# Twelve RMS norms: the inverse root moves from ScalarE and VectorE to one power operation on GpSimd

## What is computed

```python
def rmsnorm(t, g, eps=RMS_EPS):
    tf = t.astype(jnp.float32)
    tf = tf * lax.rsqrt(jnp.mean(tf * tf, axis=-1, keepdims=True) + eps)
    return (tf * g.astype(jnp.float32)).astype(t.dtype)

h = h + rmsnorm(m, g[1])                               # mixer's output
f = sq_relu_mlp(rmsnorm(h, g[2]), mlp_w1[i], mlp_w2[i])
h = h + rmsnorm(f, g[3])
```

## Time and profile before

| what | value |
|---|---|
| runs (median, lowest, highest) | 1945.8 us, 1937.51, 1949.15 |
| profiled execution, its own time | 1939.3 us |
| its span, first to last instruction | 1937.5 us |
| TensorE busy | 1656.3 us, 85% |
| VectorE busy | 1117.8 us, 58% |
| ScalarE busy | 746.8 us, 39% |
| GpSimd busy | 107.3 us, 6% |
| granted TensorE clock, mean | 0.90 |

### The profile page before, as it was taken

The page is one execution under the profiler, slowest core; times in us unless marked ns, Lnnn a source line. Parts: engine busy times, 40 slices in busy tenths (PEclk is TensorE's granted clock), DMA queues, the critical chain, the costliest instruction groups (busy, mean ns, idle before and its releaser), DMA issues. The chain is left out here.

```text
span 1937.5 us, 36240 instructions
## 1 busy us (share of the span) xinstructions
PE 1656.3 (85%) x15007; PEld 1565.6 (81%) x15007; DVE 1117.8 (58%) x1813; ACT 746.8 (39%) x1000; POOL 107.3 (6%) x139
## 2 busy tenths in 40 slices
PE   3899989947888988999887788579998889779997
PEld 2899989927878987999886786579998875579997
DVE  6995457968795556444465652654434446655444
ACT  1554345731002634554345000346533434346532
POOL 0011000002120000110000210000000020000000
PEclk7899999959999998999988696789999995589998
DMA  9897545402233454665442000225453430125551
GB/s 303 242 315 223 174 141 174 152 0 85 93 90 112 139 174 120 179 189 174 153 140 67 2 2 2 85 90 173 158 170 113 152 116 1 44 95 188 169 179 44
DMA packets 297019, 252.87 MB, mean 131 GB/s; under 512 B 9032, under 2 KB 295597, under 8 KB 296893
## 3 DMA queue, kind: packets, MB, share of 16 engines
q1 hardware_dynamic: 296589, 249.96, 42.0%
q10 hardware_dynamic: 304, 1.11, 0.1%
HBM read 249.99 MB, written 1.05 MB: 130 GB/s over the span
## 5 line engine op out<-in xcount | busy, mean ns | idle before, releaser
L399 DVE TENSOR_TENSOR w_lo<-raw,w_hi 128x2048 fp32r<-128x2048 f32 (+2 forms) x203 | 456.4, 2250 | 538.6 <-ACT w_hi L391 538.3
L466 PE MATMUL bank<-x_hi,w_hi 128*128 128x256 f32 (+1 forms) x2224 | 647.7, 291 | 72.6 <-DVE x_lo L660 41.4
L468 PE MATMUL bank<-x_hi,w_lo 128*128 128x256 f32 (+1 forms) x2224 | 639.0, 287 | 0.0
L467 PE MATMUL bank<-x_lo,w_hi 128*128 128x256 f32 (+1 forms) x2224 | 638.9, 287 | 0.0
L391 ACT ACTIVATE w_hi<-raw 128x2048 fp32r<-128x2048 f32 (+2 forms) x203 | 381.6, 1880 | 457.8 <-PE bank L468 419.3
L466 PEld LDWEIGHTS bank<-x_hi,w_hi 128*128 128x128 f32 x2224 | 428.1, 192 | 82.3 <-issue 69.7
L468 PEld LDWEIGHTS bank<-x_hi,w_lo 128*128 128x128 f32 x2224 | 429.8, 193 | 0.0
L467 PEld LDWEIGHTS bank<-x_lo,w_hi 128*128 128x128 f32 x2224 | 428.1, 193 | 0.9 <-issue 0.7
L466 PE MATMUL bank<-mh_hi,w_hi 128*128 128x272 f32 (+1 forms) x512 | 148.3, 290 | 6.5 <-PEq L2016 6.5
L467 PE MATMUL bank<-mh_lo,w_hi 128*128 128x272 f32 (+1 forms) x512 | 147.5, 288 | 0.0
L468 PE MATMUL bank<-mh_hi,w_lo 128*128 128x272 f32 (+1 forms) x512 | 147.3, 288 | 0.0
(11 more groups left out here) (432 smaller groups left out, 2160.4 us busy)
## 6 DMA issues: line engine op xcount, KB each, us to landing
raw<-in_mlp_w SPq DMA_DIRECT2D x128, 512.0 KB, 4.4
raw<-in_w_ffn_up SPq DMA_DIRECT2D x88, 512.0 KB, 5.2
raw<-in_w_ada SPq DMA_DIRECT2D x72, 512.0 KB, 4.8
raw<-in_w_in SPq DMA_DIRECT2D x60, 512.0 KB, 4.7
raw<-in_w_ffn_down SPq DMA_DIRECT2D x32, 512.0 KB, 4.5
raw<-in_od_w_in SPq DMA_DIRECT2D x24, 512.0 KB, 4.5
raw<-in_ev_w_in SPq DMA_DIRECT2D x18, 512.0 KB, 4.7
raw<-in_w_ffn_down SPq DMA_DIRECT2D x16, 384.0 KB, 3.8
```

Of the source, the lines that this page charges most:

```text
L399: nc.vector.tensor_tensor(w_lo[:, s_at % 2, 0:kt], raw[:, r_at % RING, 0:kt], w_hi[:, s_at % 2, 0:kt].bitcast(F32), ALU.subtract).then_inc ...
L466: nc.tensor.matmul(out, hi, xh[:, k0 + k, 0:L], start=start, stop=False)
L467: nc.tensor.matmul(out, hi, xl[:, k0 + k, 0:L], start=False, stop=False)
L468: mm = nc.tensor.matmul(out, lo, xh[:, k0 + k, 0:L], start=False, stop=stop)
```

## The change

`Norm` gets a method for GpSimd. After VectorE has written mean square plus epsilon, GpSimd raises it to the power minus one half in one TENSOR_TENSOR operation, whose second operand is a column filled once with -0.5 and broadcast along the row. It writes straight to where the refined root stood and raises `n_y`. The ACTIVATE of line 631 and, for these norms, the call of `inverse_root` go. VectorE waits for `n_y` as before. Each of the blocks that hold a norm gets a GpSimd part (the diff shows two of them).

```diff
+        half_neg = sb("half_neg", [P, 1])
...
+            @block.gpsimd
+            def _(pool):
+                nc.gpsimd.memset(half_neg[:], -0.5)
...
+            def on_pool(self, pool):
+
+                pool.wait_ge(n_ms, self.q + 1)
+                nc.gpsimd.tensor_tensor(stat[:, 3, 0:self.L], stat[:, 0, 0:self.L], half_neg.broadcast_to([P, self.L]), ALU.pow).then_inc(n_y, 1)
+
             def on_act(self, act, mid=None, between=None):
 
                 L = self.L
-                act.wait_ge(n_ms, self.q + 1)
-                nc.scalar.activation(stat[:, 1, 0:L], stat[:, 0, 0:L], ACT.Abs_reciprocal_sqrt).then_inc(n_y, 1)
                 if between:
                     between()
...
                 nc.vector.tensor_scalar(stat[:, 0, 0:L], banks[6][:, 0:L], 1.0 / D, EPS, ALU.mult, ALU.add).then_inc(n_ms, 1)
-                inverse_root(dve, n_y, self.q + 1, stat[:, 0, 0:L], stat[:, 1, 0:L], stat[:, 2, 0:L], stat[:, 3, 0:L])
+                dve.wait_ge(n_y, self.q + 1)
                 for n in range(DT + 2):
...
                                                     hid_hi[:, bass.ds(n, 1)].bitcast(F32), ALU.subtract).then_inc(hid_l, 1)
+                        norm.on_pool(pool)
                         each_pair(pool, FF1T, 2, body)
...
+                @block.gpsimd
+                def _(pool):
+                    if before:
+                        before.on_pool(pool)
+                    if norm:
+                        norm.on_pool(pool)
```

More of the change, by code:

```diff
@@ L905, in _ @@
                 nc.scalar.activation(sp_t[:, 2], sp_t[:, 1], ACT.Exp, scale=-1.0).then_inc(ba_act, 1)
+            @block.gpsimd
+            def _(pool):
+                norm_mix.on_pool(pool)
             @block.vector
@@ L1498, in _ @@
                         norm_in.square(act, u, sq)
+                @block.gpsimd
+                def _(pool):
+                    norm_final.on_pool(pool)
                 @block.vector
@@ L1650, in _ @@
             def _(pool):
+                norm_in.on_pool(pool)
                 pool.wait_ge(q["bon"], 1)
```

## The result

The changed kernel takes 2413.6 us (median of four runs, 2409.5 to 2416.3), the kernel before 1945.6 us beside it. The ratio is 1.242 (1.2383 to 1.2457): 468.0 us slower, where 35 us were forecast and 161 us was the upper bound. The sign was right; the change in time was wrong by a factor of thirteen.

What follows compares the result with a forecast made beforehand. TensorE's stream of products and the stretches where it stands still were taken to bound the kernel. Terms 57.9 + 8.6 - 29.6 - 1.3 - 0.5 = +35.1 us on 1939.3 gave 1974 us; range 1927 to 2100 us.

Steps and rivals of the forecast that it cites:

- The sign: Whole kernel: slower than before, by +35.1 us; slower by over 1% had chance 0.64.
- What bounds it: All twelve norms: TensorE waits, so mean square to first scaled tile is on the path one for one.
- Break-even: Twelve norms: the change breaks even where the powers cost 22.8 us in all, 1.9 us each.
- The interval before: Twelve norms of the old kernel, mean square to first scaled tile: 2.29 to 3.08 us each, sum 29.6 us.
- The interval without the power: Twelve changed norms: mean square and hand-overs to and from GpSimd, 0.71 us each, 8.6 in all (7.9 to 9.7).
- The power: GpSimd at twelve norms: 4.7 us over 256 positions, 5.0 over 272, 57.9 us in all (10.7 to 183.8).
- Rival 3: GpSimd's power: steps wait for one another, 10 us or more each; with 14.9 us, +161, 2100 us; chance 0.27.
- The other terms: Outside the norms: -1.3 us in the RWKV mixer, -0.5 in the first up loop, nothing in the second.
- the mixer's table load: RWKV mixer: load ahead of the rows TensorE awaits goes, everything behind comes 1.28 us sooner, -1.3 us.
- the up loops: Two up projections: 22 table loads go, 28 us of ScalarE's time; -0.5 us in the first, nothing in the second.
- rival 4: Up projections: table loads count for more, loops gain 28 us; with a power as cheap as a product, 1899 us; chance 0.03.
- TensorE's clock: Behind norms: a longer wait can move the return to full clock; nothing counted, 6 us either way allowed.

Runs made afterwards that it cites:

- the quarter power: Changed kernel with GpSimd raising only the first 64 positions, ScalarE and VectorE doing the others the old way: 2042.8 us against 1941.3, ratio 1.0535.

## Why the prediction was wrong, point by point

**What bounds it: right.** The interval from mean square to first scaled tile was said to be on the path one for one at all twelve norms. Three kernels with intervals of 14.0, 133.9 and 512.8 us bear that out. Only the gains of the kernels without refining steps (16.8 us of intervals for 6 and for 10 us of time) fall short of one for one. Break-even was put at 1.9 us a power: a product of 0.61 us won, the quarter power of 10.53 lost, and nothing in between was run. (The prediction says that even a free power can't win over 1%; its own -22.8 us are 1.2%, and the product in the power's place did win 1.2%.)

**The interval before: right.** 29.6 us.

**The interval without the power: a little high.** 0.71 us was counted for mean square and hand-overs, 0.54 to 0.55 was measured: 0.08 us to GpSimd rather than the 0.19 of the earlier trace rows, 0.04 back rather than 0.1. Twelve times, 2.1 us.

**The power: this step failed, and with it the whole number.** The text took 24 arithmetic steps at the price of one stream each, 0.77 ns per element, and got 4.7 and 5.0 us; and it took 24 steps at a whole product's price, 14.9 and 15.9 us, as the upper bound. Measured are 41.12 and 43.70. The term of 57.9 us is 506.3. Per element of a row that is 161 ns, 209 streams of 0.77 ns; in products of this run (0.614 us) a power is 67 of them. So neither the price of a step nor its bound held. Two things were wrong in it. The count of 24 steps came from no row, and both the forecast and the upper end of the range hung on it, so that they weren't independent; and the reasoning took the rate of products, which the earlier trace rows show as a rate of streams, for the rate at which a function of many steps is worked off. What the earlier trace rows could bound was the price from below. From above they bound nothing.

**Rival 3** (steps that wait for one another, 10 us or more) had the right direction and 0.27 of the chance, but its price was 14.9 us, not 41. Whether the steps inside the power wait for one another was not measured: no run looks inside it. For fp32 steps that depend on one another the Trainium skill (GPSIMD Engine Reference, section "Performance pitfalls for Q7 kernels") names four cycles each. At the 1.2 GHz that the Trainium skill gives there the measured 161 ns are an estimated 193 cycles for one element, or 48 such steps, twice the 24 assumed. By the three operations a cycle of the Trainium skill (same reference, section "Performance versus the Vector engine") the 24 steps would be 8 cycles, a factor of 24 below the 193. No run here tells a wrong count from a wrong rule.

**The other terms: right.** -1.3 us for the mixer's table load (1.44 us less standing in TensorE's row). Next to nothing in the up loops (0.5 us were counted): VectorE is busy for 12.97 of 13.20 us in the first, TensorE for 23.00 of 23.00 in the second. The kernel without table switches shows in the whole time that rival 4's 28 us don't exist.

**TensorE's clock: allowed for 6 us, took about 4.** The stretches between the norms moved by -6.2 us in all, 4.4 beyond the 1.8 counted for loads and the first loop; the two largest moved by -9.2 and +5.1 us and in part cancelled. That the clock made the 4.4 us is argued from its going with the lengths, and no run held it fixed. Put together with what was measured: 506.3 + 6.5 - 29.6 - 1.8 = +481.4 us, against 477.0 in the spans.

## What to carry to other kernels

An operation that no row of the profile shows isn't bounded from above by rows of other operations: where it stands twelve times on the path, its duration alone decides, and one run of it over two widths is worth more than any count of steps. GpSimd's power costs 0.16 us for each element of a row whatever the partitions and the numbers are, so at 256 elements it is 67 products, and only a row of up to five elements (1.17 us) costs less than the refining steps did (1.38 us); with the sums that short rows needed, there was no gain even then. To get rid of steps behind a root, keep the root where it is cheap (0.42 us on ScalarE), load its table ahead of need, and ask whether the refining is needed at all.

## What the runs showed of the hardware that was not expected

A power over one partition takes as long as over 128 (20.71 and 20.73 us for 128 elements), and with a base or an exponent of one no less than with any other (five pairs, 10.53 to 11.50 us at 64 elements). What spread there is goes with VectorE: a power that began under a 2.29 us operation of VectorE with two operands took longer by nearly what was left of it. The product over 256 elements shows the same, with 1.47 us where 1.00 us of such an operation was left, against 0.61 beside a quiet VectorE. The power is one instruction in the trace, with no stretch paid only by the first.

TensorE's clock makes kernels with the same work differ: one stretch of 2616 products took 278.5 to 294.2 us at a mean granted clock of 0.83 to 0.77. A gain of 16.8 us in the norms reached the end as 6. While TensorE stands for the power, the granted clock is at the lower level for nearly all of the time (0.50 to 0.56 in the mean of each of the twelve intervals), and it is not back at once (the changed kernel, same columns as the earlier trace rows: the power, the first tiles behind it, and the loop after them):

```profile
49.78:91.71 41.93, 0.00 (x0) 0.00 (x0) 0.59 (x2) 1.91 (x1) 41.12 (x1) 0.50 0.09 24
91.71:109.00 17.29, 13.80 (x83) 13.44 (x84) 17.22 (x36) 6.03 (x10) 0.00 (x0) 0.72 0.40 113
109.00:127.40 18.40, 18.40 (x159) 18.40 (x158) 17.37 (x34) 7.81 (x9) 2.30 (x3) 1.00 1.14 319
```

That costs little here, since VectorE is busy for 17.22 of those 17.29 us and sets the pace of the tiles. What decides at which moment the level changes in a long stretch, such as the mixer's, was not found, and the mean clock of one kernel differs from run to run.
